# Carrying the gate rows of a matrix-memory layer to all partitions: products with ones against a store and repeated reads

## What is computed

```python
b = jnp.cumsum(lfc, axis=1)
D = b[:, :, None, :] - b[:, None, :, :] + lic[:, None, :, :]      # masked to s <= t
inter = b + m[:, None, :]
mt = jnp.maximum(inter, jnp.max(D, axis=2))
w_inter = jnp.exp(inter - mt)
P = jnp.exp(D - mt[:, :, None, :])
A = P * jnp.einsum('bthd,bshd->btsh', qc, kc)
num = einsum(A, vc) + w_inter[..., None] * jnp.einsum('bthd,bhdv->bthv', qc, C)
carry_w = jnp.exp(b[:, -1] + m - mL)
C_new = carry_w[..., None, None] * C + jnp.einsum('bsh,bshd,bshv->bhdv', ws, kc, vc)
```

## Time and profile before

| | us |
|---|---|
| median of 3 executions | 1300.53 |
| lowest and highest | 1299.91, 1303.71 |
| the profiled execution | 1303.11 |
| its span, first to last instruction | 1301.2 |
| TensorE busy in it | 1253.4 |
| VectorE busy in it | 773.1 |
| ScalarE busy in it | 387.0 |

### The profile page before, as it was taken

One profiled execution on the slowest core, in us unless ns is written; L12 is line 12 of the kernel. 1 busy time (PEld: TensorE's weight loads), 2 busy tenths in 40 slices (PEclk: granted clock), 3 DMA queues, 4 the chain that ended last, 5 costly groups with the idle time before them and its releaser, 6 DMA issues.

```text
span 1301.2 us, 21315 instructions
## 1 busy us (share of the span) xinstructions
PE 1253.4 (96%) x9031; PEld 1192.0 (92%) x9031; DVE 773.1 (59%) x1433; ACT 387.0 (30%) x525; POOL 2.7 (0%) x7
## 2 busy tenths in 40 slices
PE   6999999999999999999999999999999999999994
PEld 5999987867999998779999999999999999999893
DVE  7632366545777886654565566766666663333766
ACT  5322132224434332112334322322222222111443
POOL 0000000000000000000000000000000000000000
PEclk9999899999999999999999999999999999999997
DMA  6223001441222323544545344121212125222212
GB/s 217 98 98 130 33 33 50 162 130 66 84 78 75 102 82 135 174 155 161 163 142 175 116 156 152 66 96 67 98 65 98 66 65 182 86 84 89 96 65 73
DMA packets 47598, 138.72 MB, mean 107 GB/s; under 512 B 4476, under 2 KB 23932, under 8 KB 38288
## 3 DMA queue, kind: packets, MB, share of 16 engines
q1 hardware_dynamic: 15896, 89.77, 20.7%
q10 hardware_dynamic: 31608, 47.60, 10.6%
HBM read 113.55 MB, written 23.81 MB: 106 GB/s over the span
## 4 chain that ended last, share of the span: by engine, by line
PE 84%; DVE 9%; ACT 3%; issue 3%; DMA 0%; DVEq 0%; ACTq 0%
PE ps L646 54%; PE ps L652 8%; PE aux L836 3%; PE ps L715 3%; PE ps L716 3%; PE ps L720 2%; PE aux L876 2%; PE aux L841 2%; PE ps L673 1%; ACT whi L1549 1%; DVE wlo L938 1%; DVE xl L1405 1%; PE aux L814 1%; PE aux L887 1%; DVE nstat L1160 1%
## 5 line engine op out<-in xcount | busy, mean ns | idle before, releaser
L646 PE MATMUL ps<-ahi,whi 128*128 128x288 f32 x1584 | 342.5, 298 | 11.9 <-DVE wlo L938 10.4
L646 PE MATMUL ps<-alo,whi 128*128 128x288 f32 x1584 | 341.2, 297 | 0.0
L938 DVE TENSOR_TENSOR wlo<-wraw,whi 128x2048 fp32r<-128x2048 f32 (+2 forms) x89 | 191.2, 2148 | 150.9 <-ACT whi L1549 150.2
L646 PEld LDWEIGHTS ps<-ahi,whi 128*128 128x128 f32 x1584 | 257.1, 190 | 13.4 <-issue 12.5
L646 PEld LDWEIGHTS ps<-alo,whi 128*128 128x128 f32 x1584 | 254.7, 189 | 0.0
L1549 ACT ACTIVATE whi<-wraw 128x2048 fp32r<-128x2048 f32 (+2 forms) x89 | 159.4, 1791 | 136.7 <-PE ps L646 121.4
L646 PE MATMUL ps<-ahi,wlo 128*128 128x288 f32 x832 | 178.9, 297 | 0.0
L646 PEld LDWEIGHTS ps<-ahi,wlo 128*128 128x128 f32 x832 | 135.0, 190 | 0.0
L652 PE MATMUL ps<-ahi,wlo 128*128 128x288 f32 x752 | 107.8, 296 | 0.0
L652 PEld LDWEIGHTS ps<-ahi,wlo 128*128 128x128 f32 x752 | 102.8, 189 | 0.0
L715 PE MATMUL ps<-whi,ahi 128*128 128x256 f32 (+1 forms) x320 | 79.4, 286 | 5.8 <-DVE vg L1230 5.8
(11 more groups left out here) (332 smaller groups left out, 1756.3 us busy)
## 6 DMA issues: line engine op xcount, KB each, us to landing
wraw<-in_w_in SPq DMA_DIRECT2D x32, 1024.0 KB, 5.2
wraw<-in_w_up SPq DMA_DIRECT2D x21, 1024.0 KB, 4.9
gate_scratch<-stg ACTq DMA_DIRECT2D x32, 288.0 KB, 3.6
gt<-gate_scratch ACTq DMA_DIRECT2D x32, 288.0 KB, 3.5
wraw<-in_w_pgate SPq DMA_DIRECT2D x6, 1024.0 KB, 4.9
wraw<-in_w_down SPq DMA_DIRECT2D x8, 704.0 KB, 4.0
wraw<-in_w_down SPq DMA_DIRECT2D x8, 640.0 KB, 3.8
st<-in_C_in ACTq DMA_DIRECT2D x4, 1024.0 KB, 6.6
```

Of the source, the lines that this page charges most:

```text
L646: mm = nc.tensor.matmul(ps[:, t % 2, a, 0:HALF], w, x[:, k, a * HALF:(a + 1) * HALF], start=f, stop=e)
L938: V.tensor_tensor(wlo[:, s, 0:n], wraw[:, s, 0:n], f32(whi[:, s, 0:n]), ALU.subtract)\
```

## The change

The rows `r1` and `ri` and the carry factors are written to DRAM once, by ScalarE's DMA queue, right after the exponentials. They come back on SP's queue by reads that repeat each row for every partition: `carry` once, and for each chunk `r1`'s part into `pw` and `ri`'s part into `qt`, in place, where VectorE takes them. `row_load` of chunk 0 is issued ahead of the load of unit `mv` 2, chunks 1 and 2 ahead of `gv` 0, chunks 3 and 4 ahead of `gv` 1. The read into `pw` waits for `att` of the chunk before (`at_ready`), the read into `qt` for the end of `m2` of the chunk before on TensorE. TensorE's products with `sel`, the constant itself and VectorE's copy to `carry` go; `m1` uses two banks instead of four, and the last stage of `rows` two instead of three. VectorE waits for `r1_in` and `ri_in` of the chunk.

```diff
+ROWS_BEFORE = {("mv", 2): (0,), ("gv", 0): (1, 2), ("gv", 1): (3, 4)}
...
     if stage[0] == "rows":
-        return 3 if stage[1] == 3 else 0
+        return 2 if stage[1] == 3 else 0
     if stage[0] == "m1":
-        return 4
+        return 2
...
+    row_s = nc.dram_tensor("row_scratch", [2, H, T], F32).ap()
+    carry_s = nc.dram_tensor("carry_scratch", [H, NC + NB], F32).ap()
...
+            def row_load(c):
+                t0, ln = chunk_span(c)
+                if c == 0:
+                    sp.wait_ge(row_out, 48)
+                    sp.dma_start(carry[:, :, :], carry_s.unsqueeze(0).broadcast_to([P, H, NC + NB]))\
+                        .then_inc(carry_in, 16)
+                else:
+                    sp.wait_ge(at_ready, c)
+                sp.dma_start(pw[0:ln, :, 0:ln], row_s[0, :, t0:t0 + ln].unsqueeze(0).broadcast_to([ln, H, ln]))\
+                    .then_inc(r1_in, 16)
+                if c:
+                    sp.wait_ge(aux_ready, job_at[("m2", c - 1)] + 2 * H)
+                sp.dma_start(qt[:, :, 0:ln], row_s[1, :, t0:t0 + ln].unsqueeze(0).broadcast_to([P, H, ln]))\
+                    .then_inc(ri_in, 16)
...
             for u, (kind, i) in enumerate(units):
                 s = u % 2
+                for c in ROWS_BEFORE.get((kind, i), ()):
+                    row_load(c)
...
-                    b = bank(j + 2)
-                    n = NC + NB
-                    for h in range(H):
-                        mm = nc.tensor.matmul(b[:, h * n:(h + 1) * n], sel[:, h, :], rowc[:, 4, :],
-                                              start=True, stop=True)
-                    mm.then_inc(aux_ready, 1)
...
-                    b = bank(j)
-                    for h in range(H):
-                        mm = nc.tensor.matmul(b[:, h * ln:(h + 1) * ln], sel[:, h, :], r1[:, t0:t0 + ln],
-                                              start=True, stop=True)
-                    mm.then_inc(aux_ready, 1)
-                    b = bank(j + 1)
-                    for h in range(H):
-                        mm = nc.tensor.matmul(b[:, h * ln:(h + 1) * ln], sel[:, h, :], ri[:, t0:t0 + ln],
-                                              start=True, stop=True)
-                    mm.then_inc(aux_ready, 1)
...
-                    b = job(j + 2)
-                    free(V.tensor_copy(carry[:, :, :].rearrange("p h c -> p (h c)"), b[:, 0:H * (NC + NB)]), j + 2)
...
-                    b = job(j)
+                    dve.wait_ge(r1_in, 16 * (c + 1))
                     for h in range(H):
 
-                        i = V.scalar_tensor_tensor(pw[0:ln, h, 0:ln], b[0:ln, h * ln:(h + 1) * ln],
+                        i = V.scalar_tensor_tensor(pw[0:ln, h, 0:ln], pw[0:ln, h, 0:ln],
                                                    colT[0:ln, c, 0, h:h + 1], nmask[0:ln, int(c == NC), 0:ln],
                                                    ALU.add, ALU.min)
+                    i.then_inc(p_pre, 1)
+                    if c == 0:
+                        dve.wait_ge(fm_ready, H)
+                        dve.wait_ge(carry_in, 16)
+                    dve.wait_ge(ri_in, 16 * (c + 1))
+                    V.tensor_tensor(qt[:, :, 0:ln], mq[:, :, t0:t0 + ln], qt[:, :, 0:ln], ALU.mult)\
+                        .then_inc(qt_ready, 1)
...
                     A.activation(rowc[:, 4, :], rowc[:, 4, :], ACT.Exp).then_inc(row_exp, 4)
+                    act.wait_ge(row_exp, 4)
+                    act.dma_start(row_s[0, :, :], r1[:, :]).then_inc(row_out, 16)
+                    act.dma_start(row_s[1, :, :], ri[:, :]).then_inc(row_out, 16)
+                    act.dma_start(carry_s, rowc[:, 4, :]).then_inc(row_out, 16)
                     act.dma_start(outs["m"], mout[:, :]).then_inc(out_done, 16)
```

More of the change, by code:

```diff
@@ L283, in build @@
         rr = at("rr", [P, T], F32, VG + 8224 + 4608)
-        sel = at("sel", [H, H, P], F32, VG + 8224 + 6912)
         QM = VG + 20480
@@ L402, in build @@
         rows_zero = sem("rows_zero")
+        row_out = sem("row_out")
+        carry_in = sem("carry_in")
+        r1_in = sem("r1_in")
+        ri_in = sem("ri_in")
         fm_ready = sem("fm_ready")
@@ L540, in _ @@
                             for n, dst in (("cmask", cmaskf[:, :, :]), ("nmask", nmask[:, :, :]),
-                                           ("sel", sel[:, :, :]), ("bmask", bmask[:, :]), ("convw", convw[:, :, :]),
+                                           ("bmask", bmask[:, :]), ("convw", convw[:, :, :]),
                                            ("convb", convb[:, :]), ("blr", blr[:, :]), ("bgate", bgate[:, :]),
@@ L556, in _ @@
                 sp.dma_start(outs["yT"][:, n, lo:hi], yt[:, n, lo:hi]).then_inc(y_out, 16)
-        NCONST = 12 * 16
+        NCONST = 11 * 16
         def raw_count(u):
@@ L795, in _ @@
                     mm.then_inc(aux_ready, 1)
-                    b = bank(j + 3)
+                    b = bank(j + 1)
                     for h in range(H):
@@ L1226, in _ @@
                             dve.wait_ge(cp_out, 16)
-                            dve.wait_ge(aux_ready, job_at[("m1", NC)] + 4)
+                            dve.wait_ge(aux_ready, job_at[("m1", NC)] + 2)
                         dve.wait_ge(tile_ready, t + 1)
@@ L1303, in _ @@
                          j + 1)
-                    b = job(j + 2)
-                    free(V.tensor_copy(carry[:, :, :].rearrange("p h c -> p (h c)"), b[:, 0:H * (NC + NB)]), j + 2)
-                    dve.wait_ge(aux_free[bank_of[j + 2]], use_of[j + 2])
+                    dve.wait_ge(aux_free[bank_of[j + 1]], use_of[j + 1])
                 elif s[0] == "m1":
@@ new lines, in _ @@
+                    if c == 0:
[4 more added lines that the diff above has]
+                        .then_inc(qt_ready, 1)
+                    b = job(j)
+                    i = V.tensor_tensor(ktok[0:ln, :, :], hv(b[0:ln, 0:H * P]), bcast(colT[0:ln, c, 1, :], P, 2),
+                                        ALU.mult)
@@ L1320, in _ @@
                     free(i, j)
                     dve.wait_ge(aux_free[bank_of[j]], use_of[j])
-                    dve.sem_inc(p_pre, 1)
+                    dve.sem_inc(kt_ready, 1)
                     b = job(j + 1)
-                    i = V.tensor_tensor(qt[:, :, 0:ln], mq[:, :, t0:t0 + ln], hv(b[:, 0:H * ln]), ALU.mult)
+                    dve.wait_ge(p_exp, c + 1)
+                    i = V.tensor_tensor(att[0:ln, :, 0:ln], pw[0:ln, :, 0:ln], hv(b[0:ln, 0:H * ln]), ALU.mult)
                     free(i, j + 1)
@@ L1326, in _ @@
                     dve.wait_ge(aux_free[bank_of[j + 1]], use_of[j + 1])
[L1327 to L1338, removed]
                     dve.sem_inc(at_ready, 1)
@@ L1660, in _ @@
                             act.wait_ge(cp_out, 16)
-                            act.wait_ge(aux_ready, job_at[("m1", NC)] + 4)
+                            act.wait_ge(aux_ready, job_at[("m1", NC)] + 2)
                         if kind == "mv" and 1 <= h <= 2 and c == 0:
@@ L1863, in constants @@
     nmask[:, 1, :][(s <= t) & (s // LS == t // LS)] = 0.0
-    sel = np.zeros((H, H, P), np.float32)
-    for h in range(H):
-        sel[h, h, :] = 1.0
     bmask = (i[:, None] % TS // LS == np.arange(NB)[None, :]).astype(np.float32)
-    return {"ident": np.eye(P, dtype=np.float32), "cmask": cmask, "nmask": nmask, "sel": sel, "bmask": bmask}
+    return {"ident": np.eye(P, dtype=np.float32), "cmask": cmask, "nmask": nmask, "bmask": bmask}
 def kernel(x_prompt, x_sample, state_mlstm_C, state_mlstm_n, state_mlstm_m, state_gla_S,
```

2 lines of the change are left out of this document (1 added, 1 removed).

## The result

The changed kernel took 1306.8 us, median of 7 runs (1305.1 to 1309.2), against 1301.4 us for the kernel before beside it (7 runs, 1299.9 to 1303.7). The ratio is 1.0040, 95% interval 1.0028 to 1.0052: 5.4 us slower, where 1.5 us less was forecast, and outside the range, which ended at 1305.0. The profiled execution took 1307.95 us (span 1306.2) against 1303.1, so the two traces differ by 4.9 us, nearly the whole of the difference of the medians.

A forecast was written before the change was run, and what follows sets the result against it. TensorE was taken to set the end in chunks 0 and 1 and the row setup, VectorE in chunks 2 to 4. Terms -4.9 + 3.4 - 3.4 + 3.4 = -1.5 us gave 1299.0 us; range 1293.5 to 1305.0.

The forecast's parts named there:

- TensorE's work that goes: Row setup and chunks 0 and 1, where TensorE sets the end: removed records and `sel` products take 4.9 us off.
- M: The moment at which `m2` of the chunk before ends on TensorE; the read into `qt` may be issued only then.
- the clock's term: Low-clock stretches: two old ones after chunks 0 and 1 go (-3.4 us), two new ones come (+3.4 us).
- VectorE's path: Chunks 2 to 4: `pw` leaves the path, the wait for `qt` joins it; 3X - 6.85, 3.4 us added.
- X: Time from M to VectorE's `qt` product: SP's reaction, the read's landing and VectorE's start; taken as 3.4 us.
- the bounds by bytes and by pieces: Landing of the `qt` read, from other reads: 2.5 us by bytes, 3.9 by pieces; the middle, 3.2, was taken.
- `pw` runs ahead: Chunks 2 to 4: `pw` waits only for the earlier `at_ready` and a weight load in chunk 3; 1.1 us leave the path.
- Costed at nothing: ScalarE's split some 2 us later, SP's issues before `mv` 2, later `gv` loads, dropped copies, fewer banks: no cost.
- TensorE's waits: Waits grow: chunk 2 from 3.2 to 6.2 us, chunk 3 from 0.65 to 3.6, chunk 4 from 0.79 to some 4.
- Old low stretches gone: After `m1` of chunks 0 and 1: both 1.2 GHz stretches, 1.7 us each, vanish with the `sel` products; 3.4 us off.
- Two new low stretches: Behind the longer waits of chunks 3 and 4: two new stretches at the lower clock, 3.4 us added.
- Rival 2: Chunks 2 to 4: short pieces make the `qt` wait outweigh the gain; 1306.1 us; chance 0.17 together with no change.

The follow-up runs named there:

- e6: Changed kernel with rows stored chunk by chunk in DRAM, one 2 KB piece per partition instead of four of 512 bytes: 1306.4 us, ratio 1.0030.
- e2: Changed kernel with a second buffer for `qt`, so its read waits for `m2` of two chunks before: 1297.1 us, ratio 0.9962.
- e10: One more profiled execution of the kernel before, nothing changed: 1301.7 us.
- e1: Changed kernel with eight unread products of constants filling TensorE's wait ahead of the first `head`: 1301.2 us, ratio 0.9995 to the kernel before.
- e7: Kernel before, without any row reads, with 7 copies of `qb` onto itself on VectorE ahead of the first `head`: 1314.3 us, ratio 1.0086.
- e8: As e7, with eight products of constants in TensorE's wait ahead of the first `head`: 1305.8 us, ratio 1.0030 to the kernel before.
- e5: Kernel before with reads for `carry` and chunk 4's rows alone, chunks 0 to 3 by products: 1311.9 us, ratio 1.0072.
- e11: One more profiled execution of the changed kernel, nothing else altered: 1309.5 us.
- e12: One more profiled execution of the same kernel as e7: 1315.6 us.
- e9: As e2, with five products of constants as fill ahead of the first `head`: 1294.4 us, ratio 0.9938 to the kernel before.
- e3: Kernel before with reads for chunks 0 and 1 and the carry factors only, products with `sel` for the rest: 1298.7 us, ratio 0.9976.

## Why the forecast was wrong, point by point

- **TensorE's work that goes, -4.9 us: right.** M of chunk 2 lies 8.5 us earlier, the 4.9 of the products and 3.6 of the two low stretches that weren't there (3.4 forecast, in the clock's term).
- **VectorE's path, +3.4 us: right in kind, too large in size.** X was 3.37, 3.24 and 3.21 us (forecast 3.4), so by the prediction's formula the term is 9.82 - 6.85 = +3.0. But from M to the end of TensorE's wait the path grew only by 0.4, 0.6 and 0.9 us, 1.9 in sum (in chunk 2: 181.19 - 166.38 = 14.8 before, 173.02 - 157.85 = 15.2 after). In chunk 2 the difference lies between the `qt` product and `att`, whose start came 2.13 us behind that product's before and 1.51 after; why is not shown. In chunk 3 the chain before ran through TensorE's own products, so a longer VectorE path counts only in part. The landing lay between the bounds by bytes and by pieces, but not because of the pieces, as e6 shows. What the Trainium skill, DMA: Bandwidth & Descriptors, section Anatomy of one DMA, states makes 2.6 us for these bytes, by an estimate; the section states it for transfers that GpSimd issues, while these are SP's, and the traces have 3.2 to 3.3. Its rule in Rules for kernel authors (issue early, wait late) holds: e2 follows it, and `qt` waits no more.
- **`pw` runs ahead: right.** It starts before M in all three chunks (156.00, 177.28 and 193.99 us). In chunk 3 it waited 2.5 us for its read, which stood behind a weight load, but VectorE was then held by `qt` in any case.
- **Costed at nothing: right.** ScalarE's later split moved one weight split by 1.8 us and nothing behind it; `gv` 0 and `gv` 1 were in time.
- **TensorE's waits: right.** 5.7, 3.4 and 3.7 us against forecasts of 6.2, 3.6 and "some 4". The stretches behind them were low, and those behind chunks 0 and 1 at 1.00, as it was put for "right".
- **Old low stretches gone, -3.4 us: right for these two traces, but no effect to count on.** e10 has the same kernel without them, and as many others elsewhere. They were put down as likely caused by the `sel` products. That these have a part in it is open (three of six traces with them, none of eight without); one trace can't tell, and with them in half the traces only, 3.4 us is more than a median can gain by it.
- **Two new low stretches, +3.4 us: the step that failed.** Places right, size wrong. In chunk 3 the stretch was 3.4 us long and the part of `m2` on the path grew by 1.5 us (198.81 to 202.52 before, 192.01 to 197.21 after), nearly as forecast. The one ahead of `head` m 0 was sized by the others as well, 1.7 us. It lasted 13.7 us and cost 5.9, and `head` m 0 took 14.6 us instead of 8.7. Behind it 3.5 more were lost (1.5 us late behind `head` m 0, 5.0 at the end). In chunk 2, where no growth was forecast, the stretch was 6.8 us long instead of 3.4 and `m2` took 0.8 us more. So the term was 0.8 + 1.5 + 5.9 + 3.5 = 11.7 us, not 3.4. The sum with the measured terms: -4.9 + 1.9 - 3.6 + 11.7 = +5.1; the two traces differ by 4.9.

The price was taken from `m2` of chunk 2, where the upper level came back 3.4 us after it had fallen, while `m2` was still running, and carried over to another stage. Chunk 3 of the changed kernel shows the same return inside `m2`:

```profile
191.60:195.00 3.40, 2.99 (x7) 2.47 (x8) 2.64 (x9) 0.39 (x1) 0.00 (x0) 0.50 0.02 5
195.00:197.20 2.20, 2.20 (x12) 1.84 (x12) 0.00 (x0) 0.77 (x2) 0.00 (x0) 1.00 0.00 0
```

In `head` m 0 it stayed away for 6.8 to 17.1 us. The two stages differ in their products and in the share of the weight loads (2.47 of 3.40 us here, 6.33 of 14.00 there); which difference matters no run tells apart. Nothing of `head` m 0 was read for the prediction but its first row.

None of the four rivals was this. Rival 2 gives nearly the right time for another reason: X was nowhere near 4.9.

**What is shown and what isn't.** Shown, by pairs that differ in the fill alone (the changed kernel and e1, e7 and e8): the unfilled wait ahead of `head` m 0 costs 5.5 and 8.5 us beyond its own length. Shown in all six traces that have a wait of 2.7 us or more there (after, e5, e6, e7, e11, e12): the lower level over much or all of `head` m 0, for 6.8 to 17.1 us; behind the 2.3 us of e2 it didn't fall. Open: why the stretches behind it (283, 314 us) come in some executions. TensorE waits 2.70 us for `vg` at 282.59 in before and at 284.37 in after, and the clock fell only in after; it fell there in e10 too. A wait of 2.2 us for `cst` in chunk 2 has a low stretch behind it in e2 and none in e9. That the later stretches follow from the first fall is not shown. How the 12.2 us of e7's median divide is seen in e12 alone: 3.4 of wait, 4.4 in `head` m 0, 4.6 behind it.

## What to carry to other kernels

A step moved from the engine that sets the end to a read that is issued when its data is wanted turns into a wait, and a wait on TensorE is to be costed with the work that stands behind it: some 3 to 4 us of idle ahead of `head` m 0 cost 5.5 and 8.5 us beyond their length, and 1.5 us in chunk 3, where the upper level came back while `m2` was still running. So a low stretch is to be priced by the stage that it will fall on; where no trace shows that stage at the lower level, the range has to hold the case that all of it runs there. Two cures worked: take the wait away with a second buffer so that the read goes out a step earlier, and, where some of it stays, fill it with products that nobody reads. And where a trace has a few short low stretches of the clock, compare two executions of the same kernel before giving a cause to any one of them.

## What the runs showed of the hardware

**Work without a gap doesn't bring the upper level back at once.** In `head` m 0 TensorE is busy without a gap by its records (14.00 of 14.00 us) and the mean granted clock is 0.52; in e11 it is 17.00 of 17.00 at 0.50, nearly 3 us of it in the dense products behind `head` m 0. In e7 and e12 the upper level came back inside the same stage, after 6.8 and 10.2 us. In `m2` of chunk 3 it took 3.4 us.

The Trainium skill, TensorE: Matmul & The Clock Gate, section HAM oscillation — how this bites in real kernels, says that a kernel whose short computation follows waits for transfers starts each time at the low level. The trace agrees at `cst` and at `head` m 0, though the waits here are for VectorE; that the low level can last over a stage of 14.6 us, which cost 5.9 us here, is what the trace adds.

**A short fill was enough.** Eight products of 128 x 128 with 256 columns, 3.45 us of the chain, kept 1.00 through the fill and the 8.7 us of `head` m 0 behind it.

**The spread of a kernel's times can be its clock.** The kernel before and e1 to e3 spread over 6 to 12 us, e9, of which there are 6 executions, over 3. The mean granted clock on record goes with the time: among the 29 executions of the kernel before beside e1 it is 0.991 or 0.992 in the four fastest (1299.3 to 1299.7 us) and 0.986 in the three slowest (1304.5 to 1305.5). The pair e7 and e12 shows it in traces. The length isn't all: the two traces of the kernel before have the same 13.7 us of low stretches ahead of the last two, at other places, and their spans differ by 1.3 us.
